# A state space mixer's gated groups: the sum of squares of a group is added up on VectorE before TensorE sums its rows

## The reference, cut to what matters

```python
    y = y.reshape(bsz, T, SSD_D_INNER) * jax.nn.silu(z.astype(f32))
    yg = y.reshape(bsz, T, G, SSD_D_INNER // G)
    yg = yg * lax.rsqrt(jnp.mean(jnp.square(yg), -1, keepdims=True) + RMS_EPS)
    y = yg.reshape(bsz, T, SSD_D_INNER) * norm_w.astype(f32)
    return y.astype(h.dtype) @ w_out
```

## Time and profile before

| | us |
|---|---|
| three runs | 3421.93, 3414.92, 3411.85 |
| their median | 3414.92 |
| the profiled execution, device time | 3413.65 |
| its span, first to last instruction | 3411.5 |
| TensorE busy | 3274.2 (96%) |
| VectorE busy | 2272.2 (67%) |
| ScalarE busy | 1820.3 (53%) |
| mean granted TensorE clock | 0.986 |

### The profile page before, as it was taken

One profiled execution on the slowest core, in us unless ns is written; L12 is line 12 of the kernel. 1 busy time (PEld: TensorE's weight loads), 2 busy tenths in 40 slices (PEclk: granted clock), 3 DMA queues, 4 the chain that ended last, 5 costly groups with the idle time before them and its releaser, 6 DMA issues.

```text
span 3411.5 us, 54971 instructions
## 1 busy us (share of the span) xinstructions
PE 3274.2 (96%) x22635; PEld 2906.2 (85%) x22635; DVE 2272.2 (67%) x3091; ACT 1820.3 (53%) x2888; POOL 482.4 (14%) x739
## 2 busy tenths in 40 slices
PE   7999999999899999999999999999999999899997
PEld 3688788788789999999999878888879988799996
DVE  3588889832644556666666676666675555799856
ACT  2344444322567646676675355555546564677644
POOL 0011111111000000000000014787120000322002
PEclk9999999999999999999999999999999999999999
DMA  9755556822234555555555545666545435455454
GB/s 350 278 177 181 185 203 217 290 99 93 93 117 143 173 180 187 192 181 187 190 181 166 179 155 198 216 218 204 172 155 171 139 124 169 152 168 169 161 175 147
DMA packets 175321, 608.44 MB, mean 178 GB/s; under 512 B 21888, under 2 KB 21920, under 8 KB 173408
## 3 DMA queue, kind: packets, MB, share of 16 engines
q1 hardware_dynamic: 145440, 495.54, 43.1%
q0 software_dynamic: 28624, 105.72, 9.1%
q10 hardware_dynamic: 1008, 3.67, 0.3%
HBM read 596.27 MB, written 8.57 MB: 177 GB/s over the span
## 4 chain that ended last, share of the span: by engine, by line
PE 76%; DVE 8%; DMA 7%; ACT 6%; issue 3%; SPq 0%; ACTq 0%; DVEq 0%
PE psum_all L587 21%; PE psum_all L583 16%; PE psum_all L585 16%; PE psum_all L580 12%; DMA raw<-in_stream 4%; DVE w_lo L517 2%; ACT w_hi L510 2%; DMA mod_early<-in_stream 1%; DVE xT L876 1%; PE psum_all L1558 1%; PE psum_all L1528 1%; DMA mod_late<-in_stream 1%; DVE ln_d L1098 1%; ACT ssd_seg L2292 1%; PE psum_all L748 1%
## 5 line engine op out<-in xcount | busy, mean ns | idle before, releaser
L587 PE MATMUL psum_all<-act_parts,w_lo 128*128 128x256 f32 (+1 forms) x6704 | 2007.7, 299 | 0.0
L517 DVE TENSOR_TENSOR w_lo<-raw,w_hi 128x1024 fp32r<-128x1024 f32 x866 | 1065.8, 1246 | 779.2 <-ACT w_hi L510 777.8
L583 PE MATMUL psum_all<-act_parts,w_hi 128*128 128x256 f32 (+1 forms) x4464 | 1408.3, 315 | 40.1 <-DVE act_parts L975 14.7
L585 PE MATMUL psum_all<-act_parts,w_hi 128*128 128x256 f32 (+1 forms) x4464 | 1378.8, 309 | 0.0
L510 ACT ACTIVATE w_hi<-raw 128x1024 fp32r<-128x1024 f32 x866 | 908.0, 1056 | 795.6 <-DMA raw<-in_stream 794.7
L587 PEld LDWEIGHTS psum_all<-act_parts,w_lo 128*128 128x128 f32 x6704 | 1282.4, 191 | 41.6
L583 PEld LDWEIGHTS psum_all<-act_parts,w_hi 128*128 128x128 f32 x4464 | 857.4, 192 | 111.7 <-issue 44.5
L585 PEld LDWEIGHTS psum_all<-act_parts,w_hi 128*128 128x128 f32 x4464 | 857.9, 192 | 43.1 <-issue 3.6
L580 PE MATMUL psum_all<-act_parts,w_hi 128*128 128x512 f32 x2240 | 798.8, 400 | 23.5 <-DVE w_lo L517 11.7
L580 PEld LDWEIGHTS psum_all<-act_parts,w_hi 128*128 128x128 f32 x2240 | 422.4, 189 | 131.0 <-issue 17.8
L876 DVE SCALAR_TENSOR_TENSOR xT<-mod_late,small,xT 128x1024 f32<-128x1024 f32 x210 | 256.6, 1280 | 8.8 <-DMA mod_late<-in_stream 6.6
(11 more groups left out here) (498 smaller groups left out, 3382.8 us busy)
## 6 DMA issues: line engine op xcount, KB each, us to landing
raw<-in_stream SPq DMA_DIRECT2D x858, 512.0 KB, 3.3
mod_late<-in_stream POOLq DMA_DIRECT2D x128, 512.0 KB, 4.6
mod_early<-in_stream SPq DMA_DIRECT2D x128, 256.0 KB, 6.3
ssd_seg<-acs_rows POOLq DMA_DIRECT2D x8, 1536.0 KB, 6.8
s_matrices<-s5p_made POOLq DMA_DIRECT2D x16, 384.0 KB, 3.7
raw<-in_stream SPq DMA_DIRECT2D x16, 256.0 KB, 4.8
s_made<-s_matrices POOLq DMA_DIRECT2D x16, 256.0 KB, 2.9
xT<-in_x SPq DMA_DIRECT2D x1, 2048.0 KB, 10.4
```

The costliest lines, as they stand in the source:

```text
L517: dve.tensor_tensor(w_lo[:, n % RING, :], raw[:, n % RING, :], w_hi[:, n % RING, :].bitcast(F32), ALU.subtract).then_inc(lo_ready, 1)
L583: pe.matmul(sums, w_hi[:, n % RING, cols], block.rhs(kk, HIGH, block.width), start=(kk == 0), stop=False)
L585: pe.matmul(sums, w_hi[:, n % RING, cols], block.rhs(kk, LOW, block.width), start=False, stop=False)
L587: last = pe.matmul(sums, w_lo[:, n % RING, cols], block.rhs(kk, HIGH, block.width), start=False, stop=(kk == block.kt - 1))
```

## The change

VectorE adds the second, third and fourth squared tile of a group to the first, in slots L+1, L+2 and L+3 (groups 0 to 6). TensorE then sums the rows of that one tile with one matmul in slot L+3, and waits there for the third addition. The root, the reciprocal and the scalings of these groups move from slot L+3 to L+4, and the split of groups 0 to 3 from L+4 to L+5. Group 7 keeps four matmuls, which now all stand in slot 81. Before, they stood in slots 79, 80, 81 and 81.

```diff
-            gated, squared, summed = (signal("ssd_" + n, 4 * G) for n in ("gated", "squared", "summed"))
+            gated, squared = (signal("ssd_" + n, 4 * G) for n in ("gated", "squared"))
+            squares_added, summed = signal("ln_added", 3 * (G - 1)), signal("ssd_summed", G + 3)
...
-            gate_at, square_at, sum_at = z_slots(1, n_in), z_slots(2, n_in), z_slots(2, n_in)
-            root_at, scale_at = slots_of(last_z, 3, n_in + 1), slots_of(last_z, 3, n_in + 1)
+            gate_at, square_at, add_at = z_slots(1, n_in), z_slots(2, n_in), z_slots(3, n_in)
+            sum_at = slots_of(last_z, 3, n_in)
+            root_at, scale_at = slots_of(last_z, 4, n_in + 1), slots_of(last_z, 4, n_in + 1)
...
-                slot = at[last_z(g)] + 4 if g < 4 else (n_in, n_in, n_in + 1, n_in + 2)[g - 4]
+                slot = at[last_z(g)] + 5 if g < 4 else (n_in, n_in, n_in + 1, n_in + 2)[g - 4]
...
-                for k in sum_at.get(slot, ()):
-                    pe.wait_ge(squared.sem, squared.at(k + 1))
-                    if k and k % 4 == 0:
-                        pe.wait_ge(rooted.sem, rooted.at(k // 4))
-                    pe.matmul(psum[7][:, 0:T], const("over_512"), sq[:, k % 4, :], start=(k % 4 == 0), stop=(k % 4 == 3)) \
-                      .then_inc(summed.sem, 1)
+                for g in sum_at.get(slot, ()):
+                    if g:
+                        pe.wait_ge(rooted.sem, rooted.at(g))
+                    if g < G - 1:
+                        pe.wait_ge(squares_added.sem, squares_added.at(3 * g + 3))
+                        pe.matmul(psum[7][:, 0:T], const("over_512"), sq[:, 0, :], start=True, stop=True) \
+                          .then_inc(summed.sem, 1)
+                    else:
+                        for k in range(4):
+                            pe.wait_ge(squared.sem, squared.at(4 * g + k + 1))
+                            pe.matmul(psum[7][:, 0:T], const("over_512"), sq[:, k, :], start=(k == 0), stop=(k == 3)) \
+                              .then_inc(summed.sem, 1)
...
                 for g in root_at.get(slot, ()):
-                    act.wait_ge(summed.sem, summed.at(4 * g + 4))
+                    act.wait_ge(summed.sem, summed.at(g + 1 if g < G - 1 else G + 3))
...
                     if k >= 4:
-                        act.wait_ge(summed.sem, summed.at(k - 3))
+                        act.wait_ge(summed.sem, summed.at(k // 4))
...
+                for k in add_at.get(slot, ()):
+                    g, j = divmod(k, 4)
+                    if j and g < G - 1:
+                        n = 3 * g + j
+                        dve.wait_ge(squared.sem, squared.at(k + 1))
+                        if j > 1:
+                            dve.wait_ge(squares_added.sem, squares_added.at(n - 1))
+                        dve.tensor_tensor(sq[:, 0, :], sq[:, 0, :], sq[:, j, :], ALU.add).then_inc(squares_added.sem, 1)
```

## The result

The changed kernel takes 3427.99 us (median of 10 runs, 3421.46 to 3436.22), the kernel before 3419.23 us in ten runs taken beside it (3411.85 to 3423.43; the three runs shown earlier were on the low side). The ratio is 1.0029, with a 95% interval of 1.0017 to 1.0040: about 10 us slower. The forecast was 3415 with 3405 to 3424, and 0.71 for no difference beyond 0.3%. The median lies 4 us above that range. The ratio does lie just inside 0.3%, but a loss that the interval sets clear of zero was not forecast.

A forecast was written before the change was run, and what follows sets the result against it. The prediction took TensorE to bound the kernel, busy 495.7 of 508 us in the stage's middle. Its terms, - 9.0 - 1.7 - 4.7 + 12.8 + 2.6 = 0.0 us, gave 3415 us, range 3405 to 3424.

The forecast's parts named there:

- I take no fall: After the new waits of 1.75 to 2.6 us at the sums, the clock was taken to stay up: 0 us.
- Sums removed: TensorE's row sums drop from 32 to 11; 21 at 0.427 us each make 9.0 us less.
- Waits that go: TensorE's wait for convolved c in L+4 goes, 4.7 us less; four waits for squares go, 1.7 us less.
- The wait in slot L-1: TensorE's wait at the end of slot L-1 stays in all seven groups, since w_lo is no earlier than the square.
- The wait that comes: At the end of L+3 TensorE waits for the third addition, behind w_lo and taps: 12.8 us more over seven groups.
- The bound of one more us a group: Upper bound on the wait for the third addition: about one us more in each of six groups if weights land late.
- the clock's: Rival: the clock falls after the new wait in each of six groups, + 9.6 us, 3424 to 3425; chance 0.05.
- the 12 us that I called short waits: In the stage's middle, the 12 us of 508 in which TensorE is not busy were called short waits.
- ScalarE's heap in L+5: Silu's table load and the split ahead of L+5's shifts delay w_lo at L+7 in groups 0 to 3: 2.6 us more.
- The end of the stage: Group 6's Sqrt moves from slot 79 to 80 with nothing of TensorE's behind it: 0 us.
- The heap at 22 us: Rival: nothing hides ScalarE's moved work in L+5; 22 us in place of 2.6, + 19.5, 3434; chance 0.09.
- the faster rival: Rival: VectorE's last addition is ready when TensorE comes, so 12.8 us falls away; 3400 to 3402; chance 0.14.

The follow-up runs named there:

- the filler: The change with four matmuls of a constant tile, result unused, issued by TensorE ahead of its wait for the third addition; stage 443.8 us, ratio 1.0012 to the kernel before.
- the kernel without the wait: The change with all additions kept, but TensorE's one sum takes only the fourth squared tile, awaiting its square; stage 428.7 us, ratio 0.9979 to the kernel before.
- the kernel with two tiles: The change with VectorE adding only tiles 1 and 2 to tile 0; TensorE sums that tile and the fourth; stage 432.2 us, ratio 0.9970 to the kernel before.
- the kernel with group 6's root in slot 81: Two tiles summed, split at L+7, and group 6's root and scale in slot 81 instead of 80; stage 426.3 us, ratio 0.9977 to the kernel before.
- the kernel with the later broadcast: The change with the 1.5 MB decay-row broadcast issued behind group g-2's row sum, not group g-1's products; stage 453.0 us, ratio 1.0042 to the kernel before.

## Why the prediction was wrong, by its own steps

The step that failed is the forecast's "I take no fall": it put the clock at 0 us, and the runs show 7.4 us, five falls of 1.5 us each. The second is the new wait, sized at 12.8 us, which measured 16.2. The other parts in turn:

- **Sums removed, 9.0 us**: right. 0.12 + 0.31 around an unheld sum as before, 22 instructions in place of 64.
- **Waits that go, 4.7 and 1.7 us**: right in kind, 4.4 and 1.4 by the starts (of the latter 1.0 inside the stage). The wait in slot L-1 stayed, now under L583, as said.
- **The wait that comes**: right in place, cause and order; its size failed, 12.8 forecast and 16.2 measured. I took the landing of the second weights from the kernel before, group by group. In the change they land 1.0 us later in four groups, 0.7 and 0.1 earlier in two, together 3.1 of the 3.4 us. The bound of one more us a group had been read from a row, and four groups reached it.
- **"I take no fall" of the clock**: the step that failed most. The rival priced it at 9.6 for six groups; it was 7.4 for five, and 7.0 by the filler. That "a wait of 2.6 is nearer to 1.4 than to 3.59" was no argument: the rows had nothing between the two. The clock of 1.00 in the earlier trace rows was no sign of safety either: that stretch holds the wait of 3.59 us and its fall, and still reads 1.00. The same wait is 3.6 of the 12 us that I called short waits.
- **ScalarE's heap in L+5, 2.6 us**: the mechanism was there, at the start of L+7, 4.1 us with group 5 among them, which I had let arrive 0.6 early.
- **"The end of the stage, 0 us"**: wrong by 1.4. The square of group 7's first tile waits for group 6's sum, then Sqrt's and Silu's tables are loaded ahead of the last z block, and slot 81 needs that block's place in PSUM.
- **The sum** was 0.0 where the stage shows + 14 in one execution and the ratio about + 10. The parts that failed are 3.4 + 7.4 + 1.5 + 1.4 = 13.7 us, all the same way; what the other terms missed by comes to 1.1 more. Also the median shown was 4 us under that of ten runs, which by itself moved 3415 to 3419.
- **The rivals**: the clock's happened (chance 0.05), together with a larger wait; I had treated them as exclusive. The heap at 22 us did not happen. VectorE was late, so the faster rival did not happen either; the kernel without the wait shows its price, 8.0 us of stage where 12.8 was said.

## What to carry to other kernels

Before work is moved off the bounding engine, ask in which slot its last input is made: here 0.43 us a group was saved by one addition that stood behind that slot's taps, and cost some 2.3 of waiting and 1.1 of slower clock. Let the bounding engine take the late input raw, as in the kernel with two tiles. And a wait that comes anew is to be priced with what follows on it: where the trace has a wait after which the clock fell, every new wait that is longer than those known to be harmless gets that price too, by a chance that is not small: here 16 waits in 20 between 1.83 and 2.94 us brought a fall.

## What the runs showed of the hardware

- In this stage, over all kernels here, the granted clock fell to 1.2 GHz with 16 of the 20 single waits of TensorE from 1.83 to 2.94 us, and after none of 1.79 or less. It stayed up after waits of 1.91, 2.45, 2.46 and 2.57, so length alone does not decide there. Elsewhere in the program it also fell after single waits of 1.54 us (the kernel with group 6's root in slot 81) and 1.77 us (the kernel without the wait), so 1.8 is no bound for other streams. Two waits of the kernel with the later broadcast, in order of time, and the clock behind each:

```profile
1504.06 0.46 PE L2222 MATMUL psum_all<-ssd_sq,consts 128*128 128x256 f32 x1 [1.91 <-DVE ssd_sq L2397]
...
1571.64 0.46 PE L2222 MATMUL psum_all<-ssd_sq,consts 128*128 128x256 f32 x1 [1.79 <-DVE ssd_sq L2397]
...
1504.10:1508.10 4.00, 4.00 (x19) 3.95 (x20) 2.70 (x3) 2.64 (x3) 0.53 (x1) 0.57 0.64 196
1571.70:1575.70 4.00, 4.00 (x32) 3.95 (x33) 2.60 (x3) 2.45 (x3) 0.53 (x1) 1.00 0.53 200
```

- Each fall cost 1.45 to 1.49 us in the change. Matmuls without any use, issued into the wait, kept the clock up and were worth 7 us of stage.
- In the change a 512 KB load took mostly 3.0 to 3.5 us from issue to landing, and 5.0 to 6.2 us when it was issued within 3 us behind a 1.5 MB broadcast on another queue. Some loads with no broadcast in flight took 4.1 to 4.4 us, several in a row; such a load made w_hi start 4.5 in place of 3.5 us after TensorE's arrival. What sets this is not shown.
